# Moving one gate product of a gated recurrence behind the next dense tile

## What is computed

```python
h = rms_norm(x, norm_mix[l])
(m_qk, m_v, m_o, m_i, m_f, r_x, r_g, a_q, a_k, a_v, a_qi, a_ki, a_w, gates) = jnp.split(h @ w_in[l], split_at, -1)
h_m = mlstm_chunkwise(m_q, m_k, m_v, ...)          # 4 heads
r_x = causal_dwconv(r_x, rglru_conv_w[l], rglru_conv_b[l])
y_b = jax.nn.gelu(r_g) * rg_lru(r_x, ...)

def rg_lru(x, w_a, b_a, w_x, b_x, lam):            # in 8 blocks of 64 channels
    r = sigmoid(x @ w_a + b_a);  i = sigmoid(x @ w_x + b_x)
    log_a = -R_C * r * softplus(-lam);  a = exp(log_a)
    u = sqrt(-expm1(2 * log_a)) * (i * x)
    h_t = a_t * h_{t-1} + u_t
```

## Time and profile before

| | us |
|---|---|
| median of 3 runs | 3546.72 |
| lowest and highest | 3546.38, 3548.82 |
| the profiled execution | 3546.01 |
| its span (first to last instruction) | 3544.2 |
| PE busy | 3491.8 (99%) |
| DVE busy | 2166.7 (61%) |
| ACT busy | 1354.5 (38%) |

### The profile page before, as it was taken

The page is one execution under the profiler, slowest core; times in us unless marked ns, Lnnn a source line. Parts: engine busy times, 40 slices in busy tenths (PEclk is TensorE's granted clock), DMA queues, the critical chain, the costliest instruction groups (busy, mean ns, idle before and its releaser), DMA issues.

```text
span 3544.2 us, 52841 instructions
## 1 busy us (share of the span) xinstructions
PE 3491.8 (99%) x21472; PEld 2856.4 (81%) x21472; DVE 2166.7 (61%) x3052; ACT 1354.5 (38%) x1576; POOL 0.2 (0%) x4
## 2 busy tenths in 40 slices
PE   8999999999999999999999999999999999999998
PEld 6778778888877787788888778888888778888887
DVE  6888567876388875687763656653233567652233
ACT  6455433322274654333222433233222443332223
POOL 0000000000000000000000000000000000000000
PEclk9999999999999999999999999999999999999999
DMA  4222224553232222345532341133322330133222
GB/s 131 81 73 71 79 95 160 176 197 129 86 95 87 72 71 73 119 143 190 189 119 86 94 131 38 50 108 102 99 95 86 94 131 27 62 113 100 95 95 71
DMA packets 273310, 364.46 MB, mean 103 GB/s; under 512 B 22636, under 2 KB 218976, under 8 KB 271840
## 3 DMA queue, kind: packets, MB, share of 16 engines
q1 hardware_dynamic: 247856, 311.34, 27.5%
q10 hardware_dynamic: 25264, 50.43, 4.1%
HBM read 351.79 MB, written 9.96 MB: 102 GB/s over the span
## 4 chain that ended last, share of the span: by engine, by line
PE 91%; DVE 5%; DVEq 2%; ACT 1%; issue 1%; DMA 0%; ACTq 0%; SPq 0%
PE banks L248 26%; PE banks L250 26%; PE banks L249 26%; PE banks L3168 1%; DVE arena L1750 1%; PE banks L3184 1%; PE banks L2099 1%; PE banks L3112 1%; PE banks L2073 1%; PE banks L2116 1%; PE banks L3061 1%; DVE w_lo L170 1%; PE banks L1385 0%; DVEq L1209 0%; DVEq L1737 0%
## 5 line engine op out<-in xcount | busy, mean ns | idle before, releaser
L248 PE MATMUL banks<-act_hi,w_hi 128*128 128x512 f32 x4064 | 1606.3, 395 | 7.0 <-DVE act_lo L533 2.5
L250 PE MATMUL banks<-act_hi,w_lo 128*128 128x512 f32 x4064 | 1583.6, 390 | 0.0
L249 PE MATMUL banks<-act_lo,w_hi 128*128 128x512 f32 x4064 | 1582.7, 389 | 0.0
L170 DVE TENSOR_TENSOR w_lo<-w_raw,w_hi 128x2048 fp32r<-128x2048 f32 (+1 forms) x280 | 629.2, 2247 | 604.6 <-ACT w_hi L164 600.5
L248 PEld LDWEIGHTS banks<-act_hi,w_hi 128*128 128x128 f32 x4064 | 763.1, 188 | 200.6 <-issue 34.3
L250 PEld LDWEIGHTS banks<-act_hi,w_lo 128*128 128x128 f32 x4064 | 762.2, 188 | 162.5
L249 PEld LDWEIGHTS banks<-act_lo,w_hi 128*128 128x128 f32 x4064 | 762.9, 188 | 157.8 <-issue 3.8
L164 ACT ACTIVATE w_hi<-w_raw 128x2048 fp32r<-128x2048 f32 (+1 forms) x280 | 526.7, 1881 | 928.6 <-PE banks L250 863.2
L2280 DVE SCALAR_TENSOR_TENSOR arena<-arena,small 128x512 f32<-128x512 f32 x168 | 126.3, 752 | 12.8
L248 PE MATMUL banks<-w_hi,act_hi 128*128 128x256 f32 x384 | 111.0, 289 | 3.6 <-DVE w_lo L170 3.6
L249 PE MATMUL banks<-w_lo,act_hi 128*128 128x256 f32 x384 | 109.3, 285 | 0.0
(11 more groups left out here) (408 smaller groups left out, 3342.8 us busy)
## 6 DMA issues: line engine op xcount, KB each, us to landing
w_raw<-in_w_in SPq DMA_DIRECT2D x98, 1024.0 KB, 5.4
arena<-in_ada_w ACTq DMA_DIRECT2D x24, 2048.0 KB, 8.1
w_raw<-in_ffn_up SPq DMA_DIRECT2D x48, 1024.0 KB, 5.3
w_raw<-in_w_gu SPq DMA_DIRECT2D x44, 1024.0 KB, 5.1
w_raw<-in_ffn_down SPq DMA_DIRECT2D x24, 1024.0 KB, 4.9
w_raw<-in_w_down SPq DMA_DIRECT2D x20, 1024.0 KB, 4.9
w_raw<-in_w_out SPq DMA_DIRECT2D x16, 1024.0 KB, 5.0
w_raw<-in_w_branch SPq DMA_DIRECT2D x12, 1024.0 KB, 5.1
```

The source lines that it names most:

```text
L170: self.core.nc.vector.tensor_tensor(view(self.lo[:, s]), view(self.raw[:, s]), view(self.hi[:, s]).bitcast(FP32), ALU.subtract)\
L248: nc.tensor.matmul(out, wh, ah, start=first, stop=False)
L249: nc.tensor.matmul(out, wh, al, start=False, stop=False)
L250: return nc.tensor.matmul(out, wl, ah, start=False, stop=last)
```

## The change

In the lists of PE, ACT and DVE, the second tile of `rx` moves one place ahead. Nothing is added, removed or resized, and the waits of each step stay as they were.

```diff
@@ pe_part
             self.dense_tile(pe, u["rx"], 0)
             value_pe(pe, 0)
+            self.dense_tile(pe, u["rx"], 1)
             lru_pe(pe, 0)
-            self.dense_tile(pe, u["rx"], 1)
             score_pe(pe, 1)
@@ act_part
             pad_act(act, 9, u["rx"], 0)
+            pad_act(act, 10, u["rx"], 1)
             lru_gates_act(act, 0)
-            pad_act(act, 10, u["rx"], 1)
             self.schedule.hi(act, u["rx"] + 1, 0)
@@ dve_part
             value_dve(dve, 0)
+            conv_dve(dve, 10, 1, "rconv", 1, A[:, self.RX + 1, :], 4, 1)
             lru_weight(dve, 0)
-            conv_dve(dve, 10, 1, "rconv", 1, A[:, self.RX + 1, :], 4, 1)
             gap_dve(dve, 1)
```

## The result

| | before | changed |
|---|---|---|
| median, us (10 runs each) | 3546.67 | 3556.44 |
| lowest and highest | 3544.35, 3550.36 | 3554.12, 3557.02 |
| the profiled execution | 3546.01 | 3556.70 |

The two medians differ by 9.8 us. The ratio on record is 1.0023, with a 95% interval of 1.0015 to 1.0031, which is 8.2 us (5.3 to 11.0); this ratio and those further down are not the quotients of the medians, which would give 1.0028 here. So the kernel became slower, by 8 to 10 us. The forecast was 5.7 us, for 3552.4. The range ended at 3556.0, and this median lies just above it. With all the runs of this study together the changed kernel has a median of 3556.0 (32 runs) and the one before 3547.8 (114 runs), a difference of 8.2.

A forecast was written before the change was run, and what follows sets the result against it. PE bounds the kernel, busy 3491.8 of 3544.2 us. Later starts of L1382 (2.25 and 0.2 us) plus 1.6 us of slow clock per layer add 5.65 us, for a median of 3552.4; range 3547.5 to 3556.

The forecast's parts named there:

- The removed waits: At L1409, the gate products' waits for the convolution, 1.57 us in layer 0 and 2.16 in layer 1, both disappear.
- the old stall: Waits at L1409 plus the slow clock behind layer 1's: 1.6 and 3.7 us, 5.2 us in all to be won.
- The new wait: At L1382, head 1's row product waits 3.97 us for ACT's sigmoids; it starts 2.25 us later in layer 0, 0.2 in layer 1.
- What costs nothing: DVE's gaps start 1.9 us later, but head 1's probabilities, weight rounding and transfers still cause PE no further wait.
- The clock: Half clock behind each new wait, over head 1's products or tile 2: 1.6 us lost per wait, bounds 0 and 2.1.
- The rival with the long slow clock: Clock stays low for two stretches behind each new wait, 3.5 us lost each, 3556.2 us in all; chance 10%.
- The range and chances: Whole kernel: 3547.5 to 3556 us; 87% within 0.2% (7.1 us) of before, about 11% slower, 2% faster.

The follow-up runs named there:

- the split tile: Kernel before with tile 1 of rx cut, 9 matrix instructions ahead of the gate products and 15 behind them: 3542.44 us against 3548.30.
- the two partial kernels: Against before, only PE's order changed: 3553.47 us; against the changed kernel, a one-element sigmoid between ACT's tile copies loads the table early: 3552.34 us.
- run 40: Not a follow-up run: "run" is a verb here, for 40 products of two columns each (L466) in the profile of the kernel before.

## Where the prediction was right, and where not

- **The removed waits.** Right. L1409 has no idle time before it in any profile of the changed kernel, and the old stall was worth 5.2 us, as the split tile shows.
- **The new wait.** Right in place, releaser and size: 3.97 us forecast, 3.94 measured, in both layers. The lengths on ACT held to within 0.05 us (copy, 0.15, load, sigmoids). Two small errors cancelled: the copy started 0.10 us after the gate products (210.66 - 210.56) and not 0.21, and PE followed the sigmoids by 0.14 us (215.49 to 215.63) and not 0.05. L1382 came 2.1 us later in layer 0, where the forecast had 2.25, and 0.06 in layer 1 (12.85 after head 0's values instead of 12.79), where it had 0.2; the gates' floor of 2.97 plus 0.97 for ACT's order is what the two partial kernels show.
- **What costs nothing.** Right. The gaps started at 219.74 (219.5 forecast, 0.4 of that being the later start of the place), the probabilities were ready well ahead, and no wait appeared further on. With the wait filled, no other wait of PE came up, and with it covered only the 0.75 us at head 1's values.
- **The clock.** Right that it falls, wrong in size, and this is the term that failed: "I take 1.6 for each wait, and keep 0 and 2.1 for the range". It took 2.6 us on average, and from 1.6 to 3.3. The 1.6 came from a wait of 2.16 us. The upper end came from the one profile of the wait of 4.8 us, in which 2.5 us of the slow stretch fell into the wait itself; in the changed kernel's profile the same wait had nearly all of its 6.8 us over work (1046.0 to 1052.7 above), 3.4 us lost. So a single row was taken for a bound. With 2.6 the sum is 2.45 + 5.2 = 7.7 us, or 3554.4 by the median known then, and with the starts as measured (2.1 + 0.06) it is the 7.4 us of the places.
- **The rival with the long slow clock** was in part what happened. It put the point from which it decides at 2.35 us lost for each wait, and 2.6 was measured; its 3.5 for each wait was nearly reached in single places (3.3). It had 10% and deserved about as much as the forecast.
- **The range and chances.** The result is at the edge of both: 9.8 or 8.2 us, by which comparison one takes, against the 7.1 up to which I gave 87%. What came lies beyond that bound, where I had put about 11%.

## What to carry to other kernels

Before a product is moved behind other work to wait less, look at who reads its result and what then stands between the two: here the cover of the next wait was moved away with it, and a wait of 1.6 to 2.2 us became one of 3.9. Where both the input of a step and its reader need cover, cut the neighbouring tile and put a part on each side. Count a stall of PE with the slow clock behind it, and take that price from several stalls or several profiles, since one profile shows only one of its values.

## What was not expected of the hardware

Behind a wait of the same 3.94 us the granted clock was at half for 3.4 us in two of eight places and for 6.8 us in six, of which 5.2 to 6.8 us were over work, and it cost 1.6 to 3.3 us. Behind waits of 2.12 to 2.16 us at L1409 it was 3.4 us in all three places, and behind the waits of 1.57 and 1.81 us there it did not fall. A wait thus cost up to 0.8 of its own length again, and the amount differed from execution to execution with the same program.

The length of a wait is not all that counts. In the profile of the kernel before, PE was never idle from 1176.0 to 1967.7, and yet the clock was at half for the last 6.7 us of it. Ahead of the fall and into it run 40 products with two columns each (L466, 1958.03 to 1963.93). What sets the clock's fall is thus not fully known from these runs:

```profile
1176.00:1960.90 784.90, 784.90 (x3857) 1.00 0.36 119
1961.00:1967.70 6.70, 6.70 (x28) 0.50 0.52 157
```
